# The mLSTM heads of a hybrid decoder step, run between the column tiles of their own input projection

## What is computed

```python
h @ w_in -> a_q a_k a_v a_g a_lr | b_q b_f b_i b_g | c_q c_k c_v c_o c_i c_f
o_a, o_b = gated_linear_recurrence(...)        # GLA and HGRN2 heads: "linear" below
# mLSTM, 4 heads of 128 x 128, per chunk of the sequence:
m_t = maximum(log_prev, max(log_d)); d = exp(log_d - m_t)
qk  = einsum(q, k) * d
num = qk @ v + w_prev * (q @ C);  den = sum(qk) + w_prev * (q . n)
h_c = num / maximum(|den|, exp(-m_t))
C   = w_old * C + (w_s * k)^T v                # and n likewise
o_c = sigmoid(c_o) * rmsnorm(h_c)
mix = concat(o_a, o_b, o_c) @ w_out            # 8 row tiles by 8 column tiles
```

## Time and profile before

| | us |
|---|---|
| timed runs | 2336.44, 2348.5, 2351.26 (median 2348.5) |
| the profiled execution | 2341.11 |
| its span, first to last instruction | 2339.4 |
| TensorE busy | 2238.8 (96%) |
| GpSimd busy | 943.5 (40%) |
| VectorE busy | 882.5 (38%) |
| ScalarE busy | 791.4 (34%) |

### The profile page before, as it was taken

One profiled execution on the slowest core, in us unless ns is written; L12 is line 12 of the kernel. 1 busy time (PEld: TensorE's weight loads), 2 busy tenths in 40 slices (PEclk: granted clock), 3 DMA queues, 4 the chain that ended last, 5 costly groups with the idle time before them and its releaser, 6 DMA issues.

```text
span 2339.4 us, 45415 instructions
## 1 busy us (share of the span) xinstructions
PE 2238.8 (96%) x19753; PEld 2180.9 (93%) x19753; DVE 882.5 (38%) x1366; ACT 791.4 (34%) x1466; POOL 943.5 (40%) x781
## 2 busy tenths in 40 slices
PE   7999999999978999999999999999999699999998
PEld 7999999999967899999999999989998588999998
DVE  6333202556244733320263332153653447333113
ACT  4333322433243533232252333243332425332322
POOL 3644444433412344444444444444334024444442
PEclk9999999999988999999999999999999799999999
DMA  3333333322311333323223333323224023332232
GB/s 116 95 87 91 94 94 85 79 66 64 86 42 41 106 91 89 88 84 89 81 83 89 87 90 95 91 71 86 65 65 106 5 86 87 87 90 86 85 90 68
DMA packets 386182, 191.96 MB, mean 82 GB/s; under 512 B 31344, under 2 KB 384896, under 8 KB 385984
## 3 DMA queue, kind: packets, MB, share of 16 engines
q1 hardware_dynamic: 385984, 189.06, 29.1%
HBM read 180.26 MB, written 8.75 MB: 81 GB/s over the span
## 4 chain that ended last, share of the span: by engine, by line
PE 92%; DVE 5%; ACT 3%; issue 1%; DMA 0%; SPq 0%; POOL 0%; ACTq 0%
PE ps L748 83%; PE ps L968 1%; DVE xn_lo L1772 1%; DVE x L1786 1%; PE ps L1232 1%; ACT squares L1656 1%; PE ps L905 1%; PE ps L1159 0%; DVE y_ffn L1782 0%; PE ps L1134 0%; DVE numer L2189 0%; DVE acc L1765 0%; ACT xn_hi L1309 0%; PE ps L1168 0%; PE ps L1161 0%
## 5 line engine op out<-in xcount | busy, mean ns | idle before, releaser
L668 POOL TENSOR_TENSOR w_lo<-w_raw,w_hi 128x512 fp32r<-128x512 f32 (+1 forms) x680 | 884.9, 1306 | 1271.3 <-ACT w_hi L1298 1270.1
L748 PE MATMUL ps<-xn_hi,w_hi 128*128 128x272 f32 x3904 | 857.4, 293 | 34.6 <-DVE xn_lo L1772 25.2
L748 PE MATMUL ps<-xn_hi,w_lo 128*128 128x272 f32 x3904 | 844.1, 290 | 0.0
L748 PE MATMUL ps<-xn_lo,w_hi 128*128 128x272 f32 x3904 | 842.8, 289 | 0.0
L1298 ACT ACTIVATE w_hi<-w_raw 128x512 fp32r<-128x512 f32 (+1 forms) x680 | 415.4, 614 | 1131.5 <-PE ps L748 1067.5
L748 PEld LDWEIGHTS ps<-xn_hi,w_hi 128*128 128x128 f32 x3904 | 630.4, 190 | 56.0 <-DVE xn_lo L1772 31.4
L748 PEld LDWEIGHTS ps<-xn_lo,w_hi 128*128 128x128 f32 x3904 | 631.9, 190 | 0.2
L748 PEld LDWEIGHTS ps<-xn_hi,w_lo 128*128 128x128 f32 x3904 | 627.8, 190 | 0.0
L748 PE MATMUL ps<-h_hi,w_hi 128*128 128x272 f32 x1344 | 292.1, 288 | 0.0
L748 PE MATMUL ps<-h_lo,w_hi 128*128 128x272 f32 x1344 | 291.4, 288 | 0.0
L748 PE MATMUL ps<-h_hi,w_lo 128*128 128x272 f32 x1344 | 291.4, 288 | 0.0
(11 more groups left out here) (316 smaller groups left out, 1376.1 us busy)
## 6 DMA issues: line engine op xcount, KB each, us to landing
w_raw<-in_ffn_w_gate SPq DMA_DIRECT2D x168, 256.0 KB, 2.8
w_raw<-in_ffn_w_up SPq DMA_DIRECT2D x168, 256.0 KB, 2.9
w_raw<-in_ffn_w_down SPq DMA_DIRECT2D x160, 256.0 KB, 2.8
w_raw<-in_w_in SPq DMA_DIRECT2D x120, 256.0 KB, 2.8
w_raw<-in_w_out SPq DMA_DIRECT2D x32, 256.0 KB, 2.9
s_c<-in_state_mlstm_C SPq DMA_DIRECT2D x8, 512.0 KB, 5.5
out_c_s<-s_c SPq DMA_DIRECT2D x8, 512.0 KB, 6.1
tok_in<-in_x_prompt SPq DMA_DIRECT2D x4, 512.0 KB, 4.1
```

What stands on the lines that cost most here:

```text
L668: pool.tensor_tensor(w_lo[:, n % RING, 0:m], w_raw[:, n % RAW, 0:m], w_hi[:, n % RING, 0:m].bitcast(F32), ALU.subtract).then_inc(w_split, 1)
L748: mm = pe.matmul(pair(p)[:, a, :], w[:, q, ws], z[:, k, half(a)], start=(k == 0 and w is w_hi and z is hi), stop=(k == chunks - 1 and w is ...
```

## The change

- The tiles come in a new order: the linear heads' q, k, f, v, i first (10 tiles), then c_o, then per head c_k, c_v, c_q, and the linear heads' gates AG and BG last.
- `STEPS` now has 48 entries. The linear steps start at tile 9 instead of 14, one in the middle and one behind each tile, and the transposes of v and rows are steps of the list. The mLSTM work of a head becomes three steps, `scores`, `sums` and `outs`, and stands at tiles 24 to 29 with three steps per tile: after the row tiles c = 2, 5 and 7. The samples are `joint` and `joint_outs`. `back` of a head lies within the `outs` of the next.
- All four engines' lists are rewritten in that order. On VectorE a tile's eviction stands behind the steps of c = 2 and 5. GpSimd's `gated` and `v_exp4` come behind the splits of the output projection's first six blocks; SyncE's stores of states and loads of samples' memories stand between the loads of the last weight blocks.
- Output projection: the mLSTM heads are row tiles k = 0 to 3 and the linear heads 4 to 7; the two first may be formed while the last tile's second half runs.
- Buffers of the heads move from the region of `xn_hi` to that of `dec` and of used tiles; `k_tok` and `squares` are now kept in the key tile and in `dmat`. The wait for the stores of the samples' memories (`cs_stored`) stands at the second SwiGLU's first `h_high`.

```diff
-    TILE_AT = list(range(LINEAR)) + [t + h for t in (CO, CV, CK, CQ) for h in range(HC)]
-    NARROW = 9
+    TILE_AT = ([AQ, AK, BQ, BQ + 1, BF, BF + 1, AV, AV + 1, BI, BI + 1] + [CO + h for h in range(HC)]
+               + [t + h for h in range(HC) for t in (CK, CV, CQ)] + [AG, AG + 1, BG, BG + 1])
+    NARROW = 8
...
     STEPS = ([("level", g, r) for r in range(ROUNDS) for g in range(2)]
-             + [(kind, g, 0) for g in range(2) for kind in ("turn", "own")]
-             + [(kind, g, 0) for g in range(2) for kind in ("attend", "samples", "states")])
...
+             + [("values", 0, 0), ("turn", 0, 0), ("own", 0, 0), ("turn", 1, 0), ("own", 1, 0), ("rows", 0, 0),
+                ("attend", 0, 0), ("samples", 0, 0), ("states", 0, 0), ("attend", 1, 0), ("samples", 1, 0), ("norm", 0, 0),
+                ("states", 1, 0), ("norm", 1, 0)]
+             + [("scores", 0, 0), ("sums", 0, 0), ("outs", 0, 0),
+                ("scores", 1, 0), ("sums", 1, 0), ("outs", 1, 0),
+                ("joint", 0, 0), ("scores", 2, 0), ("sums", 2, 0),
+                ("outs", 2, 0), ("joint_outs", 0, 0), None,
+                ("scores", 3, 0), ("sums", 3, 0), ("outs", 3, 0),
+                None, None, ("last", 0, 0)])
+    FIRST, THREES = 9, 24
+    SPOTS = [(t, c) for t in range(FIRST, NPROJ) for c in ((3, 7) if t < THREES else (2, 5, 7))]
...
+            splits(B_IN + 58, B_OUT + RING)
...
+            for j in range(4):
+                gated(j)
+            wait(root_ready, HC)
             pool.tensor_tensor(v_exp4[:].rearrange("p (b v) -> p b v", v=DVC),
...
+            def scores(h, r):
...
+                if h == 0:
+                    wait(o_ln, 4)
+                    wait(rows_split, 1)
+                    wait(rows_high, 2)
+                elif h == 1:
+                    wait(combined, 1)
...
+            def outs(h, r):
+
+                q = proj[:, CQ + h, :]
                 wait(weighted, h + 1)
...
+                if h:
+                    mm = back(h - 1)
...
+            def joint(h, r):
+
+                wait(combined, 2)
+                wait(head_gated, 1)
...
+            def joint_outs(h, r):
+
+                wait(combined, 3)
+                wait(head_gated, 2)
...
                 for p in range(OPEN):
+                    if k == 0 and p < 2:
+                        wait(proj_read, NPROJ - OPEN - 1 + p)
+                    elif k == 0:
+                        wait(head_gated, HC)
...
+                elif t == NPROJ - 1:
+                    act.wait_ge(w_used, n_in + 2 * NPROJ - 1)
+                    wait(head_gated, 2)
+                    wait(sample_step, SAMPLE_GATED)
+                    mixed_high(0)
+                    mixed_high(1)
+                    wait(proj_read, evictions(AG + 1))
+                    silus((AG, AG + 1))
+                step(t, 5)
+                act_high(act, n_in + 2 * t + 7)
+                step(t, 7)
+            wait(head_gated, 3)
+            mixed_high(2)
+            wait(proj_read, evictions(BG + 1))
+            silus((BG, BG + 1))
+            wait(head_gated, HC)
+            mixed_high(3)
...
+            for t in range(FIRST, NPROJ):
+                for c in (2, 3, 5):
+                    mixer_step(t, c)
+                if t == 17:
+                    gate_rows(1)
+                elif t == 18:
+                    gate_rows(2)
+                elif t == NPROJ - 1:
+                    unit(HC - 1)
+                    mixed_low(0)
+                    mixed_low(1)
+                proj_tile(t)
+                mixer_step(t, 7)
```

More of the change, by code:

```diff
@@ L105, in program, with step_at @@
     NCT = 3
[L107 to L110, removed]
     V1 = DVC + 1
     STEPS = ([("level", g, r) for r in range(ROUNDS) for g in range(2)]
-             + [(kind, g, 0) for g in range(2) for kind in ("turn", "own")]
-             + [(kind, g, 0) for g in range(2) for kind in ("attend", "samples", "states")])
[L116 to L125, removed]
+             + [("values", 0, 0), ("turn", 0, 0), ("own", 0, 0), ("turn", 1, 0), ("own", 1, 0), ("rows", 0, 0),
[9 more added lines that the diff above has]
+    SPOTS = [(t, c) for t in range(FIRST, NPROJ) for c in ((3, 7) if t < THREES else (2, 5, 7))]
+    assert len(SPOTS) == len(STEPS)
+    def step_at(t, c):
+        return STEPS[SPOTS.index((t, c))] if (t, c) in SPOTS else None
     with ExitStack() as ctx:
@@ L1207, in norm @@
-            def norm(n, b0):
-                for j in (2 * n, 2 * n + 1):
-                    wait(o_squared, j + 1)
-                    for a in range(2):
-                        mm = pe.matmul(ps[:, b0 + 2 * (j % 2) + a, 0:HT], blk[:],
-                                       head_sq[:, j % 2, a * HT:a * HT + HT], start=True, stop=True)
-                    mm.then_inc(o_ssq, 1)
-                wait(o_ssq, 2 * n + 2)
-                pe.sem_inc(round_done, 1)
-            program_of = {"expo": expo, "pairs": pairs_c, "own": own, "out": out, "samples": samples, "norm": norm,
-                          "back": back, "out_s": out_s, "back_s": back_s}
@@ L1220, in pe_mix @@
-            for k, (kind, n) in enumerate(SEQUENCE):
-                program_of[kind](n, begin(k))
-            wait(head_gated, HC + 1)
+                mm.then_inc(joint_done, 1)
+            step_of = {"level": level, "values": turn_values, "turn": turn, "own": own_state, "rows": turn_rows,
+                       "attend": attend, "samples": attend_samples, "states": own_samples, "norm": norm, "scores": scores,
+                       "sums": sums, "outs": outs, "joint": joint, "joint_outs": joint_outs, "last": last}
@@ new lines, in between @@
+            def between(t, c):
+                if t == OPEN + 1 and c == 3:
+                    pe_pre_sum(pe, v)
+                elif t == 5 and c == 3:
+                    wait(n_arrived, 16)
+                    pe.wait_ge(rstd_ready, v + 1)
+                    pe.transpose(ps[:, 6, 0:NS], nrow[0:NS, :], ident[0:NS, 0:NS]).then_inc(n_turned, 1)
+                elif t == 5 and c == 7:
+                    small_columns()
+                elif t == 6 and c == 3:
+                    low_rank()
+                elif step_at(t, c):
+                    kind, g, r = step_at(t, c)
+                    step_of[kind](g, r)
@@ L1224, in own_samples_c @@
+            for t in range(OPEN, NPROJ):
+                proj_tile(t, lambda c: between(t, c))
             def own_samples_c(h):
```

770 lines of the change are left out of this document (366 added, 404 removed).

## The result

| | before | after |
|---|---|---|
| median us (runs) | 2345.58 (4) | 2289.97 (4) |
| the profiled execution | 2341.11 | 2289.84 |
| its span | 2339.4 | 2287.8 |
| mean granted clock of TensorE | 0.977 | 0.986 |

The ratio is 0.9772, with a 95% interval of 0.9747 to 0.9798: faster by 2.3%. The forecast was 2283 us, in a range of 2260 to 2316; the runs after lie between 2285.65 and 2299.28.

What follows compares the result with a forecast made beforehand. TensorE, busy 96%, bounds the kernel except in two dips set by a chain between engines; per layer 42.2 - 5.8 - 3.4 - 2.0 = 31.0, twice 62, gives 2279 from the profiled execution, 2286 from the median; forecast 2283 us, range 2260 to 2316.

Steps and rivals of the forecast that it cites:

- The removable 42.2: Between tile 29 and output projection: 70.4 us less 30.0 of work, plus 1.8 in the projection's first pairs, per layer.
- The known waits: New TensorE waits for other engines where the cover between interleaved steps is too short: 5.8 us a layer.
- VectorE beside GpSimd: VectorE's SBUF-only instructions in the heads' chain slowed beside GpSimd's splits: 2 us a layer taken, bounds nothing to 8.
- `joint`: `joint` and `joint_outs` wait for the previous head's `gate`, behind `combine`: 3.05 against cover of 2.25, loss 1.6 us.
- `low_rank`: Moved to half a tile behind `small_columns`; waits for VectorE's small rows, 3.7 against 3.0, loss 0.7 us.
- Start of the output projection: p = 1 waits for the eviction of tile 29, p = 2 for `gate(3)` behind it: 0.7 us.
- `own_samples_c(0)` for `v_exp4`: In the output projection behind k = 3, TensorE waits for GpSimd's `v_exp4`: 11.7 against 10.2, loss 1.5 us.
- The clock: TensorE's clock drops behind small matmuls of `joint`, `joint_outs` and `expo`: two drops of 1.7, 3.4 us a layer.
- (A): Rival: transposes and small matmuls in the heads' steps cost the clock, four more drops a layer: 2297 us, chance 0.17.
- (B): Rival: the chain, not TensorE, sets tiles 24 to 29, 17 steps waiting 1 us each a layer: 2317, chance 0.12.
- (C): Rival: TensorE stays at 1.2 GHz through tiles 24 to 29, so slower: in full 2408 us, chance 0.03.
- (D): Rival: nothing is hidden because heads wait for their tiles: about 2340 us, chance 0.03.

Runs made afterwards that it cites:

- after once more: The changed kernel run again unedited: 2289.03 us, ratio 0.9768 to the kernel before.
- the last edits: Changed kernel with `gate` inside `combine`, `head_root(0)` later, `v_exp4` behind the sixth block's split, and two splits moved: 2266.76 us, again 2267.71.
- the edit that came out 12 us lower in one run: Changed kernel with `v_exp4` put ahead of the output projection's sixth block instead of behind the four gated outputs: 2278.07 us, one run.

## Why the prediction was right, point by point

**The mechanism.** The dip was a chain, and the chain could be covered. That is shown from both sides: 72.0 us for tiles and steps after, and the dip and more than the whole gain back when the steps go behind tile 29. Of the prediction's signs the 0.8 us between tile 29 and the output projection, the 64.8 us of idle time and the 72.0 us came as said. The `back` wait for `unit` is not gone, it is 5.4 us where it was 34.7, and no window of the clock under 0.7 stands in tiles 24 to 29.

**The ledger.** From VectorE's eviction of the sixth projection tile (tile number 5) to `own_samples_c(0)`, layer 0 takes 254.05 us where it took 284.24, layer 1 255.60 where it took 284.33: 30.2 and 28.7, against the forecast's 31.0 a layer. The sum, 58.9, is 3.1 under the forecast's 62. The span fell by 51.6, so 7.3 us were lost outside of this stretch. That is the forecast's real gap: the term was in no sum. Four of the 7.3 are the draw of the two profiled executions, since the medians differ by 55.6 us (54.8 with after once more). Some 3 to 4 us stay, and 0.7 of them are seen: from VectorE's eviction of the fourth tile to that of the sixth 7.9 us pass in each layer, in every profile of a changed kernel, and 7.5 before.

**The removable 42.2.** Without the first `norm` round and the last `back`, which lie outside of the 72.0 us window, the prediction's sum for the steps is 28.5 us, with 36 of projection 64.5. TensorE was busy for 66.9, 2.4 more. From start to start the steps take 28.3, as forecast; the 144 pairs of projection take 38.6 and not 36, since the pairs next to a step take longer (the first behind it about 0.33 us, where one between pairs takes 0.25). This price of cutting the projection into pieces was in no sum.

**The known waits, forecast at 5.8 a layer, measured 8.9 together with the 2.0 of VectorE beside GpSimd, so against 7.8.**
- `carry`: 0.2 x 3 = 0.6 for 1.0. Right kind, a little shorter.
- `joint`: 0.70 for 0.8. `joint_outs`: 1.77 for 0.8. The difference of the two, 1.07, is the length that `den` got beside the split (1.25 - 0.17 = 1.08). The steps' wait was priced rightly, and one of them met the other cost. That `gate`'s place was the cause is shown by its move.
- `low_rank`: nothing for 0.7. The sum took the five small rows as one wait. TensorE's wait ends with the third of them. VectorE and TensorE after:

```profile
456.09 0.71 DVE L1946 TENSOR_TENSOR low_rows<-ps,rstd 16x544 f32<-16x544 f32 x1 [4.62 <-PE ps L929]
...
458.34 0.49 DVE L1949 TENSOR_SCALAR row_g<-row_g,bias_if 4x544 f32<-4x544 f32 x1
```

```profile
458.98 1.18 PE L939 MATMUL ps<-low_rows,wlr 16*128 16x272 f32 x4
```

  Three rows of 0.7 us end at 458.3, 2.3 us behind the last matmul of the small columns at 456.05, and the half tile covers 3.0.
- `norm(0)`: nothing for 0.3, and not followed further.
- Start of the output projection: 0.26 at the pair that reads VectorE's last tile, for 0.7; the 0.81 of `back` just ahead was not in the sum and belongs to the next term.
- `own_samples_c(0)` for `v_exp4`: 2.88 for 1.5, **the most mis-sized term**. The place and the chain were right, the durations were not: the sum took 5.3 + 1.90 from a stretch where GpSimd was alone, and measured are 7.22 + 2.37, 2.4 us more. The prediction priced the engines' contention for VectorE's side only.

**VectorE beside GpSimd, forecast 2 a layer, bounds 0 and 8.** `back` waited 1.65, 0.28 and 0.81, 2.7 in all; with the 1.1 within `joint_outs` it is 3.8, and GpSimd's own side adds 1.4. So some 5 us, inside the bounds, over the value taken. Of `back`'s waits the cause is shown by the moved splits; that `gated` and `xn_lo` held one another up only the durations say, no run moved either alone.

On this the Trainium skill ("SBUF — State Buffer", section "SBUF: two separate sides") has a lock: a VectorE instruction in a two-port mode, or with two inputs in SBUF beside a GpSimd instruction that reads SBUF, and a GpSimd instruction exclude one another for the whole instruction. This case agrees in kind: 1.11 alone, 2.07 to 2.19 beside one split, 3.44 beside two and a memset, with splits of 1.27 to 1.33 and a memset of 1.07. By that rule a `unit` of four instructions loses up to the whole length of each GpSimd instruction that it meets. Such meetings should have been counted, and not a general share taken: in a layer of after three of the four `unit`s have one.

**The clock, forecast 3.4 a layer.** In tiles 24 to 29 it stayed at 1.00 in both layers: no step there cost anything. One window dropped to 0.83 behind the wait for `v_exp4` in each layer, 1.7 us each, and layer 1 had one deeper drop in the linear part (0.67 in 1700 to 1710). The drops behind the earlier trace rows's small matmuls stayed, at 570 to 580 and 600 to 610. In layer 0 waits and new half clock are 8.9 + 1.7 = 10.6 us, and the sum had 5.8 + 3.4 + 2.0 = 11.2: the contention was under-priced and the clock over-priced by nearly as much. That it came out so close is in this part luck. 42.2 - 10.6 is 31.6 where 30.2 was measured; the 2.4 us of busy time above are more than the difference, and the other 1.0, in the kernel's favour, was not traced.

**The rivals.** (A), transposes cost the clock: excluded, by the window's 1.00 and by the doubled transposes. (Its 64 transposes of k and v are those of both layers, 32 in each.) (B), a wait of about 1 us at each step: in the 72 us TensorE is idle for 5.1, at seven places; not the case. (C) is excluded by the same clock, and (D), nothing hidden, is what the steps behind tile 29 gave, 2352, and not what the change gave.

## What to carry to other kernels

A chain of short steps costs little (8.9 us a layer here, and 1.5 with the last edits) when each of its hand-overs is laid against the independent work between two steps; write that cover down for each wait and little is left to surprise. What the lone durations of the trace before do not hold is the price of company: once the chain is moved from an empty stretch into a full one, list for each VectorE instruction on it which GpSimd instruction now runs beside it, and for each GpSimd one the reverse, and add up to one partner's length for each meeting. Then move the partner that nobody waits for, and not the one on the chain.

## What the runs showed of the hardware that was not expected

The clock of TensorE in the openings differs between executions of the same instructions. The version with the splits moved was profiled twice; windows of the norm and first tiles of layer 0 (columns as above), first one, then the other:

```profile
400.00:410.00 10.00, 7.22 (x54) 6.78 (x53) 10.00 (x18) 4.69 (x11) 5.69 (x4) 0.97 0.55 138
410.00:420.00 10.00, 9.98 (x68) 9.71 (x68) 7.94 (x22) 6.41 (x15) 0.00 (x0) 0.86 0.01 2
420.00:430.00 10.00, 7.71 (x49) 7.27 (x48) 8.41 (x13) 6.67 (x15) 5.04 (x7) 0.83 0.48 79
```

```profile
400.00:410.00 10.00, 8.03 (x62) 7.59 (x61) 9.40 (x16) 5.10 (x11) 6.82 (x5) 1.00 0.54 131
410.00:420.00 10.00, 9.15 (x69) 8.88 (x70) 9.46 (x26) 6.90 (x16) 0.00 (x0) 1.00 0.12 28
420.00:430.00 10.00, 7.69 (x59) 7.25 (x59) 8.41 (x14) 7.39 (x17) 5.05 (x7) 1.00 0.46 77
```

There TensorE waits between short runs of matmuls, and 3.4 us are lost in the one execution and none in the other. In the opening at about 1140 both lose 3.4 us, in that at about 1540 the one loses 1.7 and the other 3.4. The same holds of after: outside of the mixers and of the start it lost 11.9 us up to 1890 us in the first profiled execution and 6.8 in after once more, with the same waits. Before lost 3.4 there. These 8.5 us of difference are where most of the ledger's 7.3 went. Whether the change made such drops likelier or this execution drew more of them the runs don't settle; no run varied the openings alone. It is also why a single execution can't price an edit of 3 us: the edit that came out 12 us lower in one run had taken 2.6 us of waits away.

The other surprise is the price of two engines on SBUF at once. Four instructions that take 1.11 us alone took up to 3.8, one of them waiting for the very end of GpSimd's. Both sides pay: GpSimd's four `gated` went from 5.3 to 7.22 us beside VectorE's `xn_lo`.
